# Two attentions of a fused two-block network: their loops over scores, weights and sums reordered

## The chip, the cores and the metric

The kernel runs on one core of a Trainium2 chip. The metric is the time of one execution on the device in microseconds (us), the median of several runs. TensorE (PE) multiplies matrices into eight PSUM banks, and its clock is granted at one of two levels, 1.2 or 2.4 GHz (0.50 and 1.00 in the rows). VectorE (DVE) and ScalarE (ACT) read and write PSUM and SBUF; GpSimd (POOL) works on SBUF here and issues some of the DMAs; SyncE (SP) streams the weights.

## The reference, cut to what matters

Everything is float32, for 512 tokens of width 1024. A first network of two layers (a recurrent mixer, then an attention with a window and sinks, each followed by a feed-forward and a gated input) feeds a second of two layers (the first of them with latent attention). Only these parts are touched:

```python
# attention with sinks: 16 query heads, 4 key heads, blocks of 128 queries, window of 128
logits = einsum('bnqhgd,bnkhd->bnhgqk', qb, kw) * (dh ** -0.5)     # own block and the one before
logits = where(valid, logits, -inf)
m = maximum(max(logits, axis=-1), sink)
probs = exp(logits - m[..., None])
denom = sum(probs, axis=-1) + exp(sink - m)
out = einsum('bnhgqk,bnkhd->bnhgqd', probs, vw) / denom[..., None]

# latent attention: 16 heads, q and k of width 96, v of width 64, blocks of 128 queries
s = einsum('bhqd,bkhd->bhqk', qi, k)                                # q scaled by 96 ** -0.5
s = where(kpos[None, :] <= qpos[:, None], s, -inf)
o = einsum('bhqk,bkhd->bqhd', softmax(s), v)
```

The sines and cosines of the first attention's rotation come from an input of positions, so they are computed in the kernel.

## The kernel before, in words

The order of the work is written out by hand, as one instruction stream for each engine, with semaphores between them. There is no scheduler: an engine does what stands next in its stream and waits there. TensorE's results take turns in two groups of four banks: `product` uses banks 0 to 3 (semaphores `product_full`, `product_done`), `small` banks 4 to 7 (`small_full`, `small_done`). Whoever empties a bank counts its `done` up, and the fifth use of a group waits for the first.

**Attention with sinks (stage `at`).** A unit is one block of queries for two of the 16 heads (`e` = 0, 1), so there are 32 units, n = u // 8 being the query block. Units 0 to 7 have only their own block of keys (128 columns a head), the others 256. In its turn u TensorE computes the scores of unit u, the transposes of unit u - LAG (LAG = 3) and the weighted sums of unit u - LAG - 1, each into the next small bank. DVE scales and masks the scores into SBUF (two instructions, L2102), takes the maximum (L2106), folds the sink in (L2109), and later (`at_scale`, L2083 to L2087) adds the exponential of the sink, inverts, and scales both heads' weights in place. ACT does the exponentials, copies the transposes out (two instructions) and then the sums. Four buffers of `temporary` hold the weights of four units.

**Before that stage (`ple2`, `norm3`, `at_in`).** `ple(2)` adds the gated input to the residual. Behind it on DVE stand nine instructions that reduce the rotation's angles (L2043 to L2053); they wait for the positions, whose DMA POOL issues (L673) only once `ple2` is done. Only then does DVE come to the reciprocal that the norm's spreading on TensorE waits for (L1831). `at_in` has 12 products of 512 columns (q and k), each followed by a sum of squares (`halves`) of the product before and a `turn` (the rotation's exchange) of the one before that. The last sum and the last two turns stand ahead of `token_major`, which computes the values (64 matmul rows of 256 columns in the trace). The stage `at` waits for the last rotation and for DVE's copies of the values (L2076).

**Latent attention (stage `mla`).** A unit is one block of queries of one head: 64 units, u = 4 hd + n, and n + 1 blocks of 128 keys. TensorE's turn u holds the scores of unit u and the transposes of unit u - 3; once the last block of a head is turned (n = 3), its four weighted sums follow at once (512, 384, 256 and 128 columns), behind a wait for ACT's four copies. All of it passes through the four small banks. DVE scales and masks the scores into `temporary` (L2283, over all keys), takes the maximum (L2286), negates it (L2287), and, one unit later, inverts the sum of the exponentials (L2293) and scales the weights (L2294). ACT does the exponentials, copies the transposes to `area_b`, and copies the head's sums to `normed`.

L741 is the helper that issues every matmul, L1065 and L1146 are the transposes of the two attentions, L1403 is the helper of all ACT instructions.

## Time and profile before

| | us |
|---|---|
| runs, median of 3 | 4471.97 (4466.77 to 4472.01) |
| profiled execution, whole | 4468.67 |
| its span, first to last instruction | 4466.8 |
| stage `at`, first scores to first product behind it | 97.2 |
| stage `mla`, the same | 166.2 |

TensorE is busy for 95% of the span, at a mean granted clock of 0.963. The two attentions are stretches in which it is less busy and its clock is lower; every other long stage is dense products. The stage times are differences of the starts at 1078.88 and 1176.06, and at 2406.08 and 2572.25.

### The profile page before, as it was taken

What the parts mean: (1) busy time and instruction counts of PE and PEld (TensorE: products, weight loads), DVE (VectorE), ACT (ScalarE), POOL (GpSimd) and SP (SyncE); (2) the same over time, 40 slices, a digit from 0 to 9 for tenths busy, and PEclk for the clock granted to TensorE, in tenths of its full rate; (3) what the DMA queues carried; (4) which work ended last, traced back from release to release, by engine and by line L of the source; (5) the groups of instructions that cost most, each with busy time, mean ns of one, the idle gap of its engine ahead of it and who ended that gap; (6) DMA issues with size and microseconds to landing.
All of it is one profiled execution on the core that took longest, in us unless ns stands there. A gap on an engine that the chain in (4) does not pass through costs nothing.

```text
span 4466.8 us, 40791 instructions
## 1 busy us (share of the span) xinstructions
PE 4263.6 (95%) x15992; PEld 2735.7 (61%) x15992; DVE 1573.6 (35%) x2918; ACT 693.5 (16%) x1468; POOL 1667.7 (37%) x1520
## 2 busy tenths in 40 slices
PE   7999999998999999999998799999999989989998
PEld 3444444445544444688843368888888346837887
DVE  4431110146511101344244534324432854454332
ACT  2321110023411100100023410001000231211000
POOL 0008888300088883244400024443443033003442
PEclk9999999998999999999999899999999889989999
DMA  3114334111053442222210022222222133112222
GB/s 115 47 64 181 146 147 154 72 64 38 34 183 146 150 152 70 71 85 83 87 61 29 1 76 85 85 85 81 89 83 88 38 101 85 33 38 76 88 87 71
DMA packets 125070, 387.45 MB, mean 87 GB/s; under 512 B 37648, under 2 KB 40720, under 8 KB 111440
## 3 DMA queue, kind: packets, MB, share of 16 engines
q1 hardware_dynamic: 109568, 302.56, 20.4%
q0 software_dynamic: 15312, 82.28, 4.8%
q8 instruction: 128, 2.10, 0.2%
q14 instruction: 62, 0.51, 0.0%
HBM read 376.40 MB, written 8.39 MB: 86 GB/s over the span
## 4 chain that ended last, share of the span: by engine, by line
PE 91%; DVE 5%; ACT 2%; issue 1%; DMA 0%; POOL 0%; DVEq 0%; POOLq 0%; ACTq 0%
PE bank L741 90%; DVE temporary L2498 1%; ACT temporary L1403 1%; DVE small_columns L2286 1%; DVE temporary L2283 1%; ACT normed L1403 0%; ACT area_b L1403 0%; DVE normed L1834 0%; DMA vector_columns<-in_vectors_dram 0%; DVE temporary L2102 0%; DVE small_columns L2106 0%; PE bank L1065 0%; PE bank L1285 0%; DVE area_a L2311 0%; DVE rstd L1849 0%
## 5 line engine op out<-in xcount | busy, mean ns | idle before, releaser
L741 PE MATMUL bank<-normed,weight_ring 128*128 128x512 f32 (+2 forms) x4080 | 1514.0, 528 | 17.4 <-DVE normed L1840 5.8
L741 PEld LDWEIGHTS bank<-normed,weight_ring 128*128 128x128 f32 (+1 forms) x4080 | 780.9, 193 | 699.3 <-issue 639.4
L741 PE MATMUL bank<-area_a,weight_ring 128*128 128x512 f32 (+1 forms) x1776 | 636.4, 515 | 8.2 <-issue 8.2
L741 PEld LDWEIGHTS bank<-area_a,weight_ring 128*128 128x128 f32 x1776 | 339.3, 192 | 282.0 <-issue 259.7
L691 POOL TENSOR_TENSOR area_b<-weight_ring 128x512 f32<-128x512 f32 (+1 forms) x68 | 84.2, 1238 | 1137.8 <-issue 567.3
L741 PE MATMUL bank<-area_b,weight_ring 128*128 128x256 f32 (+3 forms) x1616 | 500.0, 457 | 5.8 <-issue 2.8
L661 POOL TENSOR_SCALAR area_b<-area_b,small_columns 128x384 f32<-128x384 f32 x336 | 416.7, 1240 | 0.0
L741 PEld LDWEIGHTS bank<-area_b,weight_ring 128*128 128x128 f32 (+2 forms) x1616 | 302.9, 188 | 178.0 <-issue 147.0
L663 POOL TENSOR_TENSOR area_b<-area_b 128x384 f32<-128x384 f32 x336 | 333.9, 994 | 28.0
L741 PE MATMUL bank<-area_b 128*128 128x256 f32 (+2 forms) x1200 | 258.7, 378 | 16.3 <-ACT area_d L1403 16.3
L691 POOL TENSOR_TENSOR area_d<-weight_ring 128x512 f32<-128x512 f32 (+1 forms) x68 | 84.2, 1238 | 447.7 <-PE bank L741 422.8
L741 PEld LDWEIGHTS bank<-area_b 128*128 128x128 f32 (+1 forms) x1200 | 214.8, 196 | 51.4 <-ACT area_d L1403 16.9
L741 PE MATMUL bank<-area_b,area_d 128*128 128x256 f32 x1056 | 239.0, 379 | 0.0
L741 PEld LDWEIGHTS bank<-area_b,area_d 128*128 128x128 f32 x1056 | 200.6, 190 | 27.3
L1403 ACT ACTIVATE area_d<-area_d 128x512 f32<-128x512 f32 (+1 forms) x104 | 57.8, 563 | 918.4 <-DVE area_d L2184 918.4
L741 PE MATMUL bank<-normed,area_d 128*128 128x256 f32 (+2 forms) x1088 | 197.9, 339 | 0.2 <-issue 0.2
L741 PE MATMUL bank<-area_b,area_a 128*64 128x128 f32 (+11 forms) x640 | 161.6, 405 | 37.7 <-ACT area_b L1403 23.6
L638 POOL DMA_DIRECT2D area_b<-in_weights_dram x48 | 28.7, 597 | 411.1 <-PE bank L741 398.7
L2205 DVE SCALAR_TENSOR_TENSOR residual<-temporary,modulations,residual 128x256 f32<-128x256 f32 x64 | 45.3, 708 | 370.9 <-ACT temporary L1403 369.8
L741 PEld LDWEIGHTS bank<-normed,area_d 128*128 128x128 f32 (+2 forms) x1088 | 156.3, 171 | 24.4 <-issue 2.9
L1878 DVE TENSOR_TENSOR residual<-residual,bank 128x512 f32<-128x512 f32 x32 | 22.0, 688 | 418.9 <-PE bank L741 418.9
L1403 ACT ACTIVATE temporary<-bank 128x256 f32<-128x256 f32 (+1 forms) x136 | 59.0, 434 | 693.9 <-PE bank L741 693.9
(277 smaller groups left out, 4629.9 us busy)
## 6 DMA issues: line engine op xcount, KB each, us to landing
weight_ring<-in_weights_dram SPq DMA_DIRECT2D x387, 512.0 KB, 4.6
weight_ring<-in_weights_dram SPq DMA_DIRECT2D x56, 1024.0 KB, 4.8
area_b<-in_weights_dram POOLq DMA_DIRECT2D x48, 1024.0 KB, 5.3
area_b<-in_weights_dram POOLq DMA_DIRECT2D x48, 512.0 KB, 6.4
weight_ring<-in_weights_dram SPq DMA_DIRECT2D x40, 384.0 KB, 4.3
weight_ring<-in_weights_dram SPq DMA_DIRECT2D x24, 256.0 KB, 4.1
low_scratch<-area_d SPq DMA_DIRECT2D x16, 256.0 KB, 2.0
area_d<-low_scratch SPq DMA_DIRECT2D x16, 256.0 KB, 2.7
```

The lines of the kernel that those rows point to most:

```text
L638: po.dma_start(w[:, 0:k * P], io["weights"][b // TILE][:, b % TILE * P:]).then_inc(ada_landed[g % 3], 16)
L661: po.tensor_scalar(scaled, part, c, None, ALU.mult).then_inc(S("pool_step"), 1)
L663: i = po.tensor_tensor(total, total, scaled, ALU.add)
L691: po.tensor_tensor(s1, w21, w22, ALU.add).then_inc(S("pool_sum"), 1)
L741: i = pe.matmul(out, lhsT, rhs, start=start, stop=stop)
L1403: return act.activation(out, in_, func, **kw)
L1878: took(tt(X[:, k, :], X[:, k, :], pbank(m0 + k)[:, :], ALU.add), m0 + k)
L2205: return stt(x, part, g, x, ALU.mult, ALU.add)
L2283: stook(stt(w, sbank(s)[:, 0:(n + 1) * P], scale, C[:, CAT["causal"] + 512 - (n + 1) * P:CAT["causal"] + 512], ALU.mult, ALU.add), s)
L2286: own(dve.tensor_reduce(SM[:, o:o + 1], w, AX, ALU.max))
L2498: own(dve.reciprocal(r, r))
```

## The change

- **Latent attention.** It no longer uses the turns of the small banks. Scores have banks 4 to 7 (unit u in 4 + u % 4), transposes banks 0 and 1, the sums of a head bank 2 or 3, with semaphores of their own. The causal mask is added by DVE in the bank, on the 128 own keys only; the maximum is taken from the bank; ACT's exponential reads the bank and carries the factor 96 ** -0.5. The four weighted sums of a head are spread: one for each of the turns u = 4 hd + 8 to 4 hd + 11, between the scores and the transposes.
- **Attention with sinks.** LAG is 5 and there are eight buffers (four in `temporary`, four in `area_d`). Mask-adding, sink and the copy of the transposes are one instruction for both heads. DVE leaves at the reciprocal; the scaling by it is POOL's (two instructions a unit), between DVE and TensorE.
- **Before it.** The positions are loaded earlier on POOL's queue, the angles are computed by DVE inside `ple(2)` (ahead of its third block), the sines by ACT inside it (ahead of the fifth), the cosines by DVE ahead of the seventh. In `at_in` the last sum of squares and the last turns stand among the matmuls of the values.

```diff
-        LAG = 3
+        LAG = 5
...
+        def at_probs(v):
+            return (TM if v % 8 < 4 else D)[:, v % 4, :]
...
+        MLAG, MLA_OUT = 3, 8
+
+        def mla_scores(u):
+            return bank[4 + u % 4]
+
+        def mla_turned(u):
+            return bank[u % 2]
+
+        def mla_output(hd):
+            return bank[2 + hd % 2]
...
+            po.dma_start(B[:, 2, :].bitcast(I32), io["positions"]).then_inc(S("positions_landed"), 16)
...
-            po.dma_start(B[:, 2, :].bitcast(I32), io["positions"]).then_inc(S("positions_landed"), 16)
+
+            for v in range(32):
+                lo = 0 if v >= 8 else P
+                po.wait_ge(S("at_one_over"), v + 1)
+                for e in range(2):
+                    w = at_probs(v)[:, 256 * e + lo:256 * e + 256]
+                    i = po.tensor_scalar(w, w, at_column("one", v)[:, e:e + 1], None, ALU.mult)
+                i.then_inc(S("at_probs"), 1)
...
+            values = []
+            for k in range(DB):
...
+                if k == 0:
+                    square_sum(11)
+                    turn(10)
+                if k == DB - 2:
+                    turn(11)
...
-            for u in range(16 * NB + MLAG):
+            for u in range(16 * NB + MLA_OUT):
                 if u < 16 * NB:
                     hd, n = u // NB, u % NB
-                    s = small()
-                    mm(sbank(s)[:, 0:(n + 1) * P], A[0:96, hd, n * P:(n + 1) * P], B[0:96, hd, 0:(n + 1) * P], True, True,
-                       small_full)
-                if u >= MLAG:
+                    if u >= 4:
+                        pe.wait_ge(S("mla_exp"), u - 3)
+                    mm(mla_scores(u)[:, 0:(n + 1) * P], A[0:96, hd, n * P:(n + 1) * P], B[0:96, hd, 0:(n + 1) * P],
+                       True, True, S("mla_scored"))
+                if u >= MLA_OUT:
+                    hd, b = (u - MLA_OUT) // NB, (u - MLA_OUT) % NB
+                    if b == 0:
+                        pe.wait_ge(S("mla_copied"), NB * hd + NB)
+                        if hd >= 2:
+                            pe.wait_ge(S("mla_stored"), hd - 1)
+                    rows = slice(64 * (hd % 2), 64 * (hd % 2) + 64)
+                    mm(mla_output(hd)[rows, b * P:], A[:, 16 + 2 * b + hd // 8, hd % 8 * 64:hd % 8 * 64 + 64],
+                       B[:, 16 + 4 * (hd % 2) + b, b * P:], b == 0, b == NB - 1,
+                       S("mla_summed") if b == NB - 1 else None)
+                if 0 <= u - MLAG < 16 * NB:
                     v = u - MLAG
-                    hd, n = v // NB, v % NB
-                    s = small()
+                    n = v % NB
                     pe.wait_ge(S("mla_probs"), v + 1)
+                    if v >= 2:
+                        pe.wait_ge(S("mla_copied"), v - 1)
                     for b in range(n + 1):
-                        i = pe.transpose(sbank(s)[:, b * P:(b + 1) * P], TM[:, v % 4, b * P:(b + 1) * P], const("ident"))
-                    i.then_inc(small_full, 1)
-                    if n == NB - 1:
-                        o = small()
-                        for j in range(NB):
-                            sdone(pe, mla_small("turned", v - 3 + j))
-                        rows = slice(64 * (hd % 2), 64 * (hd % 2) + 64)
-                        for b in range(NB):
-                            mm(sbank(o)[rows, b * P:], A[:, 16 + 2 * b + hd // 8, hd % 8 * 64:hd % 8 * 64 + 64],
-                               B[:, 16 + 4 * (hd % 2) + b, b * P:], b == 0, b == NB - 1,
-                               small_full if b == NB - 1 else None)
+                        i = pe.transpose(mla_turned(v)[:, b * P:(b + 1) * P], TM[:, v % 4, b * P:(b + 1) * P], const("ident"))
+                    i.then_inc(S("mla_transposed"), 1)
...
+            def sines():
+                act.wait_ge(S("angles"), 1)
+                own(a(B[:, 0, :], B[:, 0, :], ACT.Sin))
+                own(a(B[:, 1, :], B[:, 1, :], ACT.Sin))
+                a(B[:, 1, :], B[:, 1, :], ACT.Square).then_inc(S("sines"), 1)
+
+            ple(2, sines)
...
-                        o = 2 * (u % 4) + e
-                        p = TM[:, u % 4, 256 * e + (0 if n else 128):256 * e + 256]
-                        a(p, p, ACT.Exp, bias=SM[:, o:o + 1], accum_out=SM[:, 8 + o:9 + o]).then_inc(S("at_exp"), 1)
-                        a(SM[:, 16 + o:17 + o], vec("at_sinks", 4 * g + 2 * e + half), ACT.Exp,
-                          bias=SM[:, o:o + 1]).then_inc(S("at_exp"), 1)
+                        p = at_probs(u)[:, 256 * e + (0 if n else 128):256 * e + 256]
+                        a(p, p, ACT.Exp, bias=at_column("max", u)[:, e:e + 1],
+                          accum_out=at_column("sum", u)[:, e:e + 1]).then_inc(S("at_exp"), 1)
+                    a(at_column("sink", u), at_column("sink", u), ACT.Exp).then_inc(S("at_exp"), 1)
-                    for e in range(2):
-                        cols = slice(256 * e + (0 if v >= 8 else 128), 256 * e + 256)
-                        i = a(B[:, 12 + v % 4, cols], sbank(s)[:, cols], ACT.Identity)
-                    stook(i, s)
+                    out, turned = (x.rearrange("p (e k) -> p e k", e=2)[:, :, 0 if v >= 8 else P:]
+                                   for x in (B[:, 12 + v % 4, :], sbank(s)[:, :]))
+                    stook(a(out, turned, ACT.Identity), s)
...
+            def stored(hd):
+                rows = slice(64 * (hd % 2), 64 * (hd % 2) + 64)
+                act.wait_ge(S("mla_summed"), hd + 1)
+                a(H[rows, hd // 2, :], mla_output(hd)[rows, :], ACT.Identity).then_inc(S("mla_stored"), 1)
+
+            for u in range(16 * NB + MLA_OUT):
+                    if u >= 4:
+                        act.wait_ge(S("mla_transposed"), u - 3)
+                    a(TM[:, o, 0:(n + 1) * P], mla_scores(u)[:, 0:(n + 1) * P], ACT.Exp, scale=scale, bias=SM[:, o:o + 1],
+                      accum_out=SM[:, 4 + o:5 + o]).then_inc(S("mla_exp"), 1)
+                if u >= MLA_OUT + NB and u % NB == 0:
+                    stored(u // NB - 3)
+                if 0 <= v < 16 * NB:
+                    hd, n = v // NB, v % NB
+                    act.wait_ge(S("mla_transposed"), v + 1)
+                    if v >= 8 and n == 0:
+                        act.wait_ge(S("mla_summed"), hd - 1)
+                    a(B[:, 16 + 4 * (hd % 2):17 + 4 * (hd % 2) + n, n * P:(n + 1) * P],
+                      mla_turned(v)[:, 0:(n + 1) * P].rearrange("p (b t) -> p b t", t=P), ACT.Identity)\
+                        .then_inc(S("mla_copied"), 1)
+            stored(15)
...
+            ple(2, {2: angles, 6: cosines})
...
+            def at_one_over(v):
+                dve.wait_ge(S("at_exp"), 3 * v + 3)
+                own(tt(at_column("sum", v), at_column("sum", v), at_column("sink", v), ALU.add))
+                dve.reciprocal(at_column("one", v), at_column("sum", v)).then_inc(S("at_one_over"), 1)
...
+                    band = C[:, CAT["band"] + lo:CAT["band"] + 256].unsqueeze(1).to_broadcast([P, 2, 256 - lo])
+                    stook(stt(w, scores, 0.125, band, ALU.mult, ALU.add), s)
+                    sinks = V[:, VAT["at_sinks"] + 4 * g + half:VAT["at_sinks"] + 4 * g + half + 3:2, 0]
+                    most = at_column("max", u)
+                    own(dve.tensor_reduce(most, w, AX, ALU.max))
+                    own(tt(most, most, sinks, ALU.max))
+                    own(tt(at_column("sink", u), sinks, most, ALU.subtract))
+                    ts(most, most, -1.0, None, ALU.mult).then_inc(S("at_minus_max"), 1)
...
-                    s, w = mla_small("scores", u), TM[:, o, 0:(n + 1) * P]
-                    sfull(dve, s)
-                    if u >= 4:
-                        sfull(dve, mla_small("turned", u - 4))
-                    stook(stt(w, sbank(s)[:, 0:(n + 1) * P], scale, C[:, CAT["causal"] + 512 - (n + 1) * P:CAT["causal"] + 512],
-                              ALU.mult, ALU.add), s)
-                    sdone(dve, s)
+                    w, own_keys = mla_scores(u)[:, 0:(n + 1) * P], mla_scores(u)[:, n * P:(n + 1) * P]
+                    dve.wait_ge(S("mla_scored"), u + 1)
+                    own(tt(own_keys, own_keys, C[:, CAT["causal"] + 384:CAT["causal"] + 512], ALU.add))
-                    ts(SM[:, o:o + 1], SM[:, o:o + 1], -1.0, None, ALU.mult).then_inc(S("mla_minus_max"), 1)
+                    ts(SM[:, o:o + 1], SM[:, o:o + 1], -scale, None, ALU.mult).then_inc(S("mla_minus_max"), 1)
```

TensorE's stream in the latent attention before, from the turn of the fourth scores to the end of the first head's sums (each matmul stands once here; in the trace a float32 one has two rows, a transpose one). `area_b,area_a 64x...` are the weighted sums, `constant_matrices,temporary` the transposes:

```order
L741 MATMUL bank7<-area_b,area_a 128x512 [waits small_done3]
L1146 MATMUL bank4<-constant_matrices,temporary 128x128 [waits mla_probs,small_done0]
...
L741 MATMUL bank5<-area_b,area_a 128x384 [waits small_done1]
L1146 MATMUL bank6<-constant_matrices,temporary 128x128 [waits mla_probs,small_done2]
L1146 MATMUL bank6<-constant_matrices,temporary 128x128 x3
L741 MATMUL bank7<-area_b,area_a 64x512 [waits small_done0,small_done2,small_done3]
L741 MATMUL bank7<-area_b,area_a 64x384
L741 MATMUL bank7<-area_b,area_a 64x256
L741 MATMUL bank7<-area_b,area_a 64x128
L741 MATMUL bank4<-area_b,area_a 128x512 [waits small_done0]
```

Now, the same place one head later, where the first head's sums stand:

```order
L755 MATMUL bank4<-area_b,area_a 128x128 [waits mla_exp]
L755 MATMUL bank2<-area_b,area_a 64x512 [waits mla_copied]
L1189 MATMUL bank1<-constant_matrices,temporary 128x128 [waits mla_copied,mla_probs]
L1189 MATMUL bank1<-constant_matrices,temporary 128x128
L755 MATMUL bank5<-area_b,area_a 128x256 [waits mla_exp]
L755 MATMUL bank2<-area_b,area_a 64x384
L1189 MATMUL bank0<-constant_matrices,temporary 128x128 [waits mla_copied,mla_probs]
L1189 MATMUL bank0<-constant_matrices,temporary 128x128 x2
L755 MATMUL bank6<-area_b,area_a 128x384 [waits mla_exp]
L755 MATMUL bank2<-area_b,area_a 64x256
```

The four sums in one piece, with the fourth next scores behind them, have become one sum behind each of four scores.

TensorE at the end of `at_in` before: `squares` is the last sum of squares, `area_a` the last turns, `weight_ring,normed` the first matmuls of the values.

```order
L741 MATMUL bank6<-squares,constant_matrices 128x512 [waits at_square,small_done2]
L741 MATMUL bank7<-area_a,constant_matrices 128x512 [waits at_scaled,small_done3]
L741 MATMUL bank4<-area_a,constant_matrices 128x512 [waits at_scaled,small_done0]
L741 MATMUL bank2<-weight_ring,normed 128x256 [waits product_done2]
L741 MATMUL bank3<-weight_ring,normed 128x256 [waits product_done3]
```

Now, from the fourth of the 32 value matmuls, and again from the 28th:

```order
L755 MATMUL bank1<-weight_ring,normed 128x256 [waits product_done1]
L755 MATMUL bank6<-squares,constant_matrices 128x512 [waits at_square,small_done2]
L755 MATMUL bank7<-area_a,constant_matrices 128x512 [waits at_scaled,small_done3]
L755 MATMUL bank2<-weight_ring,normed 128x256
...
L755 MATMUL bank4<-area_a,constant_matrices 128x512 [waits at_scaled,small_done0]
L755 MATMUL bank2<-weight_ring,normed 128x256
```

The last sum and the last-but-one turn moved behind an eighth of the values, the last turn behind seven eighths.

## Rows read from the trace of the kernel before

**Rows 1.** The page: shares of the chain that ended last.

```profile
PE 91%; DVE 5%; ACT 2%; issue 1%; DMA 0%; POOL 0%; DVEq 0%; POOLq 0%; ACTq 0%
```

**Rows 2.** Windows: length, then busy us of PE, PEld, DVE, ACT, POOL; clock, DMA.

```profile
1078.88:1176.06 97.18, 90.45 (x464) 63.39 (x465) 79.67 (x288) 73.39 (x288) 0.00 (x0) 0.82 0.00 1
2406.08:2572.25 166.17, 120.88 (x416) 56.94 (x417) 97.33 (x320) 72.89 (x208) 0.00 (x0) 0.88 0.00 1
2416.00:2425.10 9.10, 6.44 (x26) 3.23 (x27) 6.08 (x21) 4.48 (x13) 0.00 (x0) 1.00 0.01 2
2455.50:2467.50 12.00, 9.34 (x27) 4.16 (x27) 6.06 (x21) 4.50 (x13) 0.00 (x0) 0.75 0.01 1
1095.00:1110.00 15.00, 15.00 (x44) 9.02 (x43) 10.40 (x37) 8.62 (x36) 0.00 (x0) 0.50 0.00 0
```

**Rows 3.** Timeline, `ple2` and norm3: start, length, engine, line, [idle before].

```profile
881.92 0.69 DVE L1889 TENSOR_TENSOR temporary<-temporary,bank 128x512 f32<-128x512 f32 x1 [7.17 <-PE bank L741]
...
941.67 0.27 ACT L1403 ACTIVATE small_columns<-bank,vector_columns 128x4 f32<-128x4 f32 x1 [4.71 <-PE bank L741]
...
944.71 0.17 DVE L1831 RECIPROCAL small_columns<-small_columns 128x4 f32<-128x4 f32 x1
```

**Rows 4.** Timeline, the end of `at_in` and the first scores.

```profile
1042.25 7.03 PE L741 MATMUL bank<-normed,weight_ring 128*128 128x512 f32 x16
...
1055.18 2.04 PE L741 MATMUL bank<-area_a,constant_matrices 128*128 128x512 f32 x2 [1.93 <-DVE area_a L2063]
1061.15 2.05 PE L741 MATMUL bank<-area_a,constant_matrices 128*128 128x512 f32 x2 [3.93 <-DVE area_a L2063]
1062.99 15.17 PE L741 MATMUL bank<-weight_ring,normed 128*128 128x256 f32 x64
...
1076.90 1.72 DVE L2076 COPY area_a<-bank 128x256 f32<-128x256 f32 x4 [11.65 <-PE bank L741]
...
1078.88 1.24 PE L741 MATMUL bank<-area_a 64*128 64x128 f32 x16 [0.71 <-DVE area_a L2076]
```

**Rows 5.** Stage `at`: timeline, chain (start, length, what), and POOL's group.

```profile
1083.37 0.66 PE L1065 MATMUL bank<-constant_matrices,temporary 128*128 128x128 f32 x2 [3.26 <-DVE temporary L2087]
...
1105.67 3.05 PE bank L741 x8
1108.72 1.04 PE bank L1065 x4
...
1117.25 0.59 PE bank L1065 x4
1117.84 2.08 PE bank L741 x12
...
1164.82 0.81 PE L741 MATMUL bank<-area_a 64*128 64x256 f32 x3
...
1176.06 2.38 PE L741 MATMUL bank<-area_b,weight_ring 128*128 128x512 f32 x5 [0.67 <-ACT area_b L1403]
...
L661 POOL TENSOR_SCALAR area_b<-area_b,small_columns 128x384 f32<-128x384 f32 x336 | 416.7, 1240 | 0.0
```

**Rows 6.** Stage `mla`: timeline, then groups (count, busy us, mean ns, idle before).

```profile
2416.01 3.39 PE L741 MATMUL bank<-area_b,area_a 128*64 128x512 f32 x10 [1.46 <-ACT area_b L1403]
...
2419.45 0.69 DVE L2283 SCALAR_TENSOR_TENSOR temporary<-bank,constant_matrices 128x512 f32<-128x512 f32 x1 [2.60 <-PE bank L741]
...
2455.46 6.31 PE L741 MATMUL bank<-area_b,area_a 128*64 128x512 f32 x10 [1.46 <-ACT area_b L1403]
...
L2283 DVE SCALAR_TENSOR_TENSOR temporary<-bank,constant_matrices 128x512 f32<-128x512 f32 x16 | 11.1, 692 | 55.2 <-PE bank L741 55.2
...
L2286 DVE TENSOR_REDUCE small_columns<-temporary 128x1 f32<-128x512 f32 x16 | 11.0, 686 | 0.5
...
L2293 DVE RECIPROCAL small_columns<-small_columns 128x1 f32<-128x1 f32 x64 | 9.8, 153 | 0.4 <-ACT temporary L1403 0.4
...
L2283 DVE SCALAR_TENSOR_TENSOR temporary<-bank,constant_matrices 128x128 f32<-128x128 f32 x16 | 4.6, 286 | 0.8 <-PE bank L741 0.8
```

142 lines of the change are left out of this document (52 added, 90 removed).

## The prediction

> **What bounds the kernel now.** I read four views in this order. The chain of waits gives TensorE 91% of the span and DVE 5% [rows 1]: outside the attentions there is nothing for this change to shorten, and DVE's share is where to look. The windows by stage then price the two attentions: 97.2 us for the one with sinks, at a mean clock of 0.82, and 166.2 us for the latent one, at 0.88, with TensorE busy for 120.9 us of it, DVE 97.3 and ACT 72.9 [rows 2]. No engine fills the latent stage, so it is bound by waits. The timeline shows which: behind the fourth scores of a head TensorE runs ten rows in one piece for 3.39 us, eight of weighted sums and two of the next 512-wide scores [rows 6]. It was let in by ACT's copy after 1.46 us of idling, and DVE, whose next mask-add needs those scores, sat idle for 2.60 us in front of it. A head takes 9.10 us at the full clock and 12.00 where the same ten rows took 6.31 at a clock of 0.75 [rows 2, 6]. Last, the timeline of the two joints: DVE's reciprocal in norm3 comes 2.77 us after ACT's root [rows 3], and TensorE stops twice for a turn before it may begin the values [rows 4].
>
> **The change, part by part.**
>
> *The angles.* The root ends at 941.67 + 0.27 = 941.94; the reciprocal starts at 944.71, when DVE has done its nine instructions on angles [rows 3]. With these gone it starts at about 942.0: 2.7 us less. They now stand in `ple2`, where DVE idles for 7.17 us before each block [rows 3]; nine instructions at no more than the 0.69 of the mask-wide one there come to 6.2 [rows 3], so the idle time covers them. If it did not, the price would be their excess once. ACT gets sines and changes of table there; the covers of both are alike. POOL was free long before, so the earlier DMA of positions waits for nobody. I take 2.7, between 0 and 2.8.
>
> *The end of `at_in`.* Values take 15.17 us for eight steps of rows, 1.90 a step; a 512-wide product of two rows costs 0.86 to 0.88 (7.03 for 16, the first group ends with its drain) [rows 4]. The sixteen rows end at 1042.25 + 16 x 0.43 = 1049.1, a sum of squares and a turn behind them at 1050.8. From there: step one to 1052.7, the last sum of squares to 1053.6, then the turn waits for DVE as before and starts at 1055.18 [rows 4], ends at 1056.0; six steps to 1067.4, the last turn to 1068.3. DVE then needs 2.1 us for the last rotation and 1.72 for its four copies [rows 4], which end at 1072.2; they used to end at 1078.6. The scores of stage `at` start 6.4 us earlier. TensorE no longer waits for the second turn's 3.93 us, and the first one's 15 us of values cover the rest. What is late next is the rotation, now behind the last turn. Bounds: 4 (both waits gone and nothing else) to 7.2 (values at full clock throughout).
>
> *Attention with sinks.* TensorE is the bound through most of it: a unit with 256 keys costs 0.59 for transposes and 2.08 for sums and scores at the full clock, 1.04 and 3.05 at the lower one, where only half the sums stand [rows 5]. The change does not take a row from it. DVE loses two scalings and the doubled instructions, ACT one instruction in each of three places; neither was the bound until near the end. Fill: before, 4.5 us from the first scores to the first transposes, with 3.26 idle [rows 4, 5]. Now two more units of scores go in ahead, but the path has POOL's two scalings in it. Net 0.5 us less. Drain: from the last scores, 1164.82 + 0.81, to the product behind it at 1176.06 there are 10.4 us [rows 5]; work in them is four groups of transposes (2.4) and five of sums (5.1), and 0.7 for ACT's last copy. The longer queue lets it run through: 2.2 us less. Against that stands the clock. It was at its lower level from 1083 to 1117 though TensorE was never idle (15 us out of 15 busy at 0.50 in the middle of it), and was up in the first turn with eight rows of sums [rows 2, 5]. That turn now comes two units of scores later (LAG 5), each 1.0 us dearer at the lower clock: 2.0 us more. Sum 0.7 less.
>
> POOL's scaling of 128x256 has no row. A 128x384 one on POOL takes 1.24 us [rows 5], so two take under 2.48; against a unit of 2.67 it is hidden, with five units of lead. Below, in proportion, it is 0.83 each. I take 0.85.
>
> *Latent attention.* DVE works 9.10 - 2.60 = 6.50 us a head. Mask-adding shrinks from 692 to 286 ns in the widest unit, evenly less in the others (0.41 + 0.27 + 0.14): 0.81 less, so 5.70 [rows 6]. The maximum over the bank has no row; over SBUF it takes 686 ns, and a DVE instruction that reads the bank at the same width 692 [rows 6], so I price it alike; a tenth more would give 5.9. ACT has 4.5 to 4.6 a head [rows 2]. TensorE: above, the 6.44 busy us of a head at full clock [rows 2], drains included; below, 3.39 + 1.29 for the narrower scores (768 columns, by the 0.43 of a 512-column row) + ten transposes by 0.59 / 4 = 1.48 [rows 4, 5, 6], in all 6.16. I take 6.2, 1.55 a unit. TensorE becomes the bound, DVE close behind. Nothing waits for a whole head any more: the sums of a head start five turns after its last scores, and their copies come two turns earlier.
>
> Fill: until the turn of the first sum the loop goes by DVE, 0.5 + 7 x 5.70 / 4 = 10.5 us. Then 55 turns of 1.55: 85.3. Drain: behind the last turn come the last unit's maximum, exponential, scaling, four transposes, copy, the last head's sums (2.3) and their copy, in all 6.7. The fill leaves TensorE half idle, which is where its clock has fallen in this stage; I add 3 us for one such spell (the ten rows cost 2.9 more at the lower clock [rows 6]). Sum 105.5 instead of 166.2: 60.7 less.
>
> *Sum.* 2.7 + 6.4 + 0.7 + 60.7 = 70.5 us. The profiled execution took 4468.7, and the median of the runs is 3.3 above it. So 4398.2 for an execution like that one, 4401.5 for the median; I say 4401.
>
> **The rivals.**
>
> *The lower clock keeps coming back in the latent stage.* Seven of its sixteen heads now take 9.10 us or close to it, the others 10.4 to 12.1, and the slower ones have a clock of 0.75 to 0.83; one of each kind is in [rows 2]. If it did so in half the heads after the change, each would cost 6.2 + 2.9 + 1.29 = 10.4 instead of 6.2, and the time would be 4401 + 8 x 4.2 = 4435. For it: in stage `at` a TensorE that was never idle stayed at the lower level for over 30 us [rows 2, 5]. Against it: in the latent stage the clock fell where TensorE idled for waits, and these go; scores and sums now form an even stream of 640 columns a turn.
> The Trainium skill (TensorE: Matmul & The Clock Gate, section "A second HAM failure mode: psum-queue depth-cycling") says that a loop which goes through PSUM banks with short idle moments between its groups of matmuls has its clock swing between both levels; this loop does that, and by that rule this rival is the outcome. The stretch of stage `at` after 1117, also short groups over four banks, kept the full clock, which speaks against the rule here.
>
> *DVE and ACT in series.* DVE's reciprocal waits for the exponential of the unit before, and with it the next unit's mask-add is stuck. If each unit paid for it (mask 0.32, maximum 0.55, negation 0.2, exponential 0.65, inversion and scaling 0.5: 2.2 us), the 64 would take 141 and the whole 4401 + 40 = 4441. Against it: 64 such waits came to 0.4 us before [rows 6], and each unit still has the next one's mask and maximum between.
>
> *The clock rises early in stage `at`.* The rotation's idle is gone, and TensorE may start its units warm. Eight small units would gain 0.9 each and five large ones 1.3: 4387. Little speaks for it, since the first transposes still wait some 4 us.
>
> *Slower than before.* If the small matmuls of both attentions never let the clock rise, stage `at` pays from its thirteenth unit on 2 x 2.08 + 1.04 = 5.2 instead of 2.67, eighteen times: 46 us; the latent stage takes 16 x 10.4 + 12 = 178, 12 more than before; the joints give back 9. In all 4472 + 49 = 4521. It decides from the latent stage alone being at the lower level throughout (about equal to before); every unit of stage `at` beyond four makes it slower.
>
> **How the numbers follow.** The forecast has 0.75, the swinging clock 0.10, the series 0.06, the early clock 0.05, the slower case 0.03; 0.01 is left for a transfer or wait that I have not seen and that eats everything. The forecast's own range is 4388 to 4416: 5.70 a head as the pace and no spell would give 10 less, 6.44 four more, half the joints 5 more. To hold 8 in 10 with the two dearer cases near 4435, I say 4385 to 4434. A measurement of this kernel tells from no change about 0.2%, 9 us. Faster 0.96, same 0.01, slower 0.03.
>
> **What would show it.** Right: norm3's reciprocal within 0.2 us of the root; values starting before the last two turns, with one wait of 1.6 us; stage `at` 96 us long, with a low clock until its fifteenth turn; POOL's scalings under 1.0 us; a latent stage of 100 to 110 us at a clock above 0.95, TensorE idle under 5%, DVE at about 90%. Wrong: a clock near 0.75 in the latent stage, DVE idle before its reciprocals, or a maximum over the bank dearer than 0.75 us for 512 columns.

## The result and the profile after

The changed kernel takes 4398.37 us (median of 4 runs, 4395.47 to 4400.04) against 4470.55 us for the kernel before (4 runs): a ratio of 0.9841, 95% interval 0.9829 to 0.9854. I had said 4401. The profiled execution has a span of 4398.2 us, 68.6 less than before. Cut at five places that both programs pass, the difference is:

| stretch | before | after | forecast |
|---|---|---|---|
| start to norm3's root | 941.67 | 941.35 | 0 |
| root to first scores of `at` | 137.21 | 126.38 | -9.1 |
| `at` | 97.18 | 96.64 | -0.7 |
| `at_out` to `mla` | 1230.02 | 1230.99 | 0 |
| `mla` | 166.17 | 108.65 | -60.7 |
| `mla_out` to the end | 1894.55 | 1894.19 | 0 |

The sum is -0.32 - 10.83 - 0.54 + 0.97 - 57.52 - 0.36 = -68.60.

The page of the changed kernel gives the shares of the chain that ended last:

```profile
PE 94%; DVE 3%; ACT 2%; issue 0%; DMA 0%; POOL 0%; DVEq 0%; ACTq 0%; POOLq 0%
```

DVE went from 5% of the chain to 3 [rows 1]. The change is real: the whole interval of the ratio lies under 1. The windows of the two attentions, and behind them one head of the latent one (length, then busy us of PE, PEld, DVE, ACT, POOL, granted clock, DMA share, GB/s):

```profile
1067.73:1164.37 96.64, 91.79 (x465) 64.32 (x465) 62.80 (x224) 64.95 (x224) 53.29 (x64) 0.79 0.00 1
2395.36:2504.01 108.65, 105.50 (x416) 46.42 (x416) 86.31 (x320) 71.62 (x208) 0.00 (x0) 1.00 0.00 1
2410.64:2417.23 6.59, 6.59 (x27) 2.87 (x27) 5.65 (x23) 4.64 (x15) 0.00 (x0) 1.00 0.00 0
```

In `mla` TensorE is busy for 97% of the stage at the full clock; before it was 73% at 0.88 [rows 2]. Of the 57.5 us gained, 42.1 are idle time of TensorE (45.3 before, 3.2 now) and 15.4 are busy time, which shrank because no row runs at the lower clock any more. A head takes 6.59 us, and TensorE has no idle time in it. In `at` the mean clock has fallen from 0.82 to 0.79, and POOL has taken 53 us of work.

The joints, in the timeline of the changed kernel (start, length, engine, line, what, idle time before and its releaser):

```profile
941.35 0.26 ACT L1436 ACTIVATE small_columns<-bank,vector_columns 128x4 f32<-128x4 f32 x1 [4.71 <-PE bank L755]
941.65 0.18 DVE L1872 RECIPROCAL small_columns<-small_columns 128x4 f32<-128x4 f32 x1 [5.73 <-ACT small_columns L1436]
...
1038.85 7.03 PE L755 MATMUL bank<-normed,weight_ring 128*128 128x512 f32 x16
...
1051.78 1.10 PE L755 MATMUL bank<-area_a,constant_matrices 128*128 128x512 f32 x2 [1.60 <-DVE area_a L2108]
...
1052.72 10.52 PE L755 MATMUL bank<-weight_ring,normed 128*128 128x256 f32 x48
...
1063.08 1.02 PE L755 MATMUL bank<-area_a,constant_matrices 128*128 128x512 f32 x2
...
1066.07 1.41 DVE L2121 COPY area_a<-bank 128x256 f32<-128x256 f32 x4
...
1067.73 2.41 PE L755 MATMUL bank<-area_a 64*128 64x128 f32 x20 [1.91 <-DVE area_a L2121]
```

The reciprocal follows the root by 0.30 us instead of 3.04 [rows 3]. One turn is waited for, 1.60 us; the other, at 1063.08, has no wait. Of the two waits of 1.93 and 3.93 us [rows 4] the second is gone. A new one stands in front of the first scores, 1.91 us where it was 0.71 [rows 4], since the rotation and the copies come behind the last turn.

The first transposes of `at` on TensorE, the turn in which its clock rises, and POOL's scalings (in the view of one line: duration ns min/median/max):

```profile
1072.99 0.66 PE L1096 MATMUL bank<-constant_matrices,temporary 128*128 128x128 f32 x2 [1.47 <-POOL temporary L686]
...
1106.13 1.11 PE L1096 MATMUL bank<-constant_matrices,temporary 128*128 128x128 f32 x4
1107.18 1.97 PE L755 MATMUL bank<-area_b,area_a 128*64 128x128 f32 x8
1109.08 1.29 PE L755 MATMUL bank<-area_a 64*128 64x256 f32 x4
1110.29 0.66 PE L1096 MATMUL bank<-constant_matrices,temporary 128*128 128x128 f32 x4
```

```profile
L686 POOL TENSOR_SCALAR temporary<-temporary,small_columns x32: 597/924/927, 1071.7 to 1148.3; 128x256 f32<-128x256 f32 x24, 128x128 f32<-128x128 f32 x8
```

Four transposes take 1.11 us before that turn's sums and 0.66 behind it; in the kernel before, the chain has 1.04 and 0.59 for them [rows 5]. The low clock ends with the scores that start at 1109.08, 41.4 us into the stage. In the kernel before it ended with those at 1115.69, 36.8 us into it, also in the first turn with eight rows of sums:

```profile
1113.79 1.97 PE L741 MATMUL bank<-area_b,area_a 128*64 128x128 f32 x8
1115.69 1.56 PE L741 MATMUL bank<-area_a 64*128 64x256 f32 x4
```

POOL's scaling of 128x256 takes 924 ns.

In `mla`, first a stretch of TensorE's timeline, then DVE's groups over thirteen heads (count, busy us, mean ns, idle time before):

```profile
2443.43 0.33 PE L1189 MATMUL bank<-constant_matrices,temporary 128*128 128x128 f32 x1
2443.59 1.39 PE L755 MATMUL bank<-area_b,area_a 96*128 96x128 f32 x4
2444.91 0.44 PE L1189 MATMUL bank<-constant_matrices,temporary 128*128 128x128 f32 x2
2445.19 1.39 PE L755 MATMUL bank<-area_b,area_a 96*128 96x256 f32 x4
```

```profile
L2316 DVE TENSOR_TENSOR bank<-bank,constant_matrices 128x128 f32<-128x128 f32 x53 | 15.7, 296 | 9.5 <-PE bank L755 9.5
L2317 DVE TENSOR_REDUCE small_columns<-bank 128x1 f32<-128x512 f32 x13 | 9.0, 692 | 0.4
```

A turn is a group of transposes, then two rows of scores and two of one block's sums. The mask-add in the bank costs 296 ns, the maximum over the bank 692, and DVE waits 9.5 us in 85 for scores. Before, the waits in front of the widest unit's mask-add alone came to 55.2 us in the stage [rows 6].

### The profile page after: what moved, and what is told of

The parts are those of the page before. It is cut to its first block, busy times and chain, and to the rows that moved or that the text cites. A ratio compares the mean times of both kernels' runs of the same rounds, so it can differ in the third digit from the quotient of the medians.

```text
span 4398.2 us, 40701 instructions
## 1 busy us (share of the span) xinstructions
PE 4247.2 (97%) x15992; PEld 2725.3 (62%) x15992; DVE 1546.4 (35%) x2854; ACT 683.6 (16%) x1404; POOL 1722.9 (39%) x1584
## 4 chain that ended last, share of the span: by engine, by line
PE 94%; DVE 3%; ACT 2%; issue 0%; DMA 0%; POOL 0%; DVEq 0%; ACTq 0%; POOLq 0%
PE bank L755 92%; DVE temporary L2529 1%; PE bank L1189 1%; ACT normed L1436 0%; PE bank L1096 0%; DVE normed L1875 0%; DMA vector_columns<-in_vectors_dram 0%; ACT temporary L1436 0%; ACT area_b L1436 0%; DVE rstd L1890 0%; PE bank L1318 0%; DVE area_a L2342 0%; ACT squares L1436 0%; ACT L1436 0%; DVE temporary L2040 0%
## 5 line engine op out<-in xcount | busy, mean ns | idle before, releaser
L755 PE MATMUL bank<-area_b 128*128 128x256 f32 (+2 forms) x1200 | 258.6, 378 | 16.2 <-ACT area_d L1436 16.2
L755 PE MATMUL bank<-normed,area_b 128*128 128x256 f32 x704 | 166.3, 379 | 0.0
L755 PE MATMUL bank<-area_b,area_a 128*64 128x128 f32 (+11 forms) x640 | 148.8, 374 | 13.2 <-DVE area_b L2033 9.8
```

Of the source, the lines that this page charges most:

```text
L755: i = pe.matmul(out, lhsT, rhs, start=start, stop=stop)
```

## The experiments

Eleven of the twelve kernels below have the same instructions in front of norm3's root as the changed one (experiment 2 moves the angles), and yet this part took from 932.93 us in one of them to 941.35 in the changed kernel, each in its profiled execution, with the clock's low spells in other places. So a part worth a few us is read from the length of its stage, and the time of the whole kernel is the second witness.

**1. The latent part as before.**

```
-            for u in range(16 * NB + MLA_OUT):
+            for u in range(16 * NB + MLAG):
...
+                    if n == NB - 1:
+                        o = small()
+                        for j in range(NB):
+                            sdone(pe, mla_small("turned", v - 3 + j))
...
-                    own(tt(own_keys, own_keys, C[:, CAT["causal"] + 384:CAT["causal"] + 512], ALU.add))
+                    stook(stt(w, sbank(s)[:, 0:(n + 1) * P], scale, C[:, CAT["causal"] + 512 - (n + 1) * P:CAT["causal"] + 512],
+                              ALU.mult, ALU.add), s)
```

> The changed kernel with the latent attention alone put back: mask-add over the full width into SBUF, the four weighted sums of a head in one piece behind its last transposes, all in the four banks used in rotation. The joints and the attention with sinks stay changed. If the two attentions don't influence each other, the stage is 166 us long again instead of 108.6 and the time is 4398.4 + 57.5 = 4456, ratio to the kernel before 0.9967. Rival: part of the 57.5 us comes from TensorE entering the stage in a better state than before (it waits 0.88 us there); then the stage stays well under 166 (say 150) and the time under 4441.

Measured: 4457.48 us, ratio 0.9978 (0.9968 to 0.9987). Window of the stage:

```profile
2392.70:2561.24 168.54, 123.31 (x416) 57.98 (x417) 97.30 (x320) 72.88 (x208) 0.00 (x0) 0.86 0.00 1
```

The whole gain of the stage goes with its code; the rival is out. The low clock comes back too: the ten rows behind the fourth scores took 6.31 us in one head and 3.40 in the next.

**2. The joints as before.**

```
-            ple(2, {2: angles, 6: cosines})
+            ple(2)
...
-                if k == 0:
-                    square_sum(11)
-                    turn(10)
-                if k == DB - 2:
-                    turn(11)
```

> The changed kernel with the angles back in front of norm3's reciprocal, and the values of at_in back behind the last two turns. Both attentions stay changed. My steps say 2.7 us for the angles and 7.8 for the end of at_in, so that the first scores of the attention with sinks start 10.8 us later and the time is about 4409, ratio 0.9864. Rival: the joints' gain is given back at the start of the attention with sinks, because TensorE's clock falls there after the wait for the last rotation: with only 0.7 us of waiting there, as before, the clock would stay up for longer, the stage would be some us shorter than 96.6, and the time under 4404.

Measured: 4402.45 us, ratio 0.9855 (0.9838 to 0.9871). From the root to the first scores it is 138.25 us, 11.9 more than in the changed kernel, and the stage behind is 4.3 longer, not shorter:

```profile
1074.34:1175.30 100.96, 94.36 (x464) 65.72 (x465) 62.71 (x224) 64.83 (x224) 53.30 (x64) 0.78 0.00 1
```

The two add up to 16.2 us, of which the whole kernel shows 4.1: against them stand 5.3 us in front of the root (where DVE and ACT no longer have the angles) and 3.8 and 4.2 in the long stretches behind the two attentions, whose code is unchanged; `mla` took 1.1 more. The clock did fall later (7 us into the stage instead of in its first), but it also rose later, at 51 us instead of 41. The rival had the first half right and the second wrong. Its time, under 4404, did come true, but by the spells elsewhere and not by a shorter stage.

Against the kernel before, which differs from this one in the attention with sinks as well, the stage is 3.8 us longer (100.96 for 97.18). So behind the old joints the changed attention costs time.

**3. The attention with sinks as before.**

```
-        LAG = 5
+        LAG = 3
...
-                    at_one_over(u - 1)
+                    at_scale(u - 1)
```

> The changed kernel with the attention with sinks alone put back: transposes three turns behind the scores, the scaling on DVE, one instruction for each half in the mask-add and in ACT's copy. Theory: this part of the change is worth half a microsecond, since TensorE bounds the stage and its lower clock costs as much as the filled drain gives: stage 97 us against 96.6, low clock until the twelfth turn instead of the fourteenth, time 4399, ratio 0.984. Rival: the old form would pay for an earlier start of the scores with waits on DVE, and the stage is 100 us or more.

Measured: 4395.12 us, ratio 0.9836 (0.9821 to 0.9851).

```profile
1064.18:1163.23 99.05, 92.65 (x464) 64.77 (x465) 79.72 (x288) 73.36 (x288) 0.00 (x0) 0.79 0.00 1
```

In its stage the change is worth 2.4 us; the kernel's own time, 3 us lower than with the change, doesn't show it: 3.5 us less in front of the root and 4.2 less in the long stretch behind the stage outweigh it. The turns with the first eight sums, at a lag of three:

```profile
1099.09 1.97 PE L739 MATMUL bank<-area_b,area_a 128*64 128x128 f32 x8
...
1104.04 1.97 PE L739 MATMUL bank<-area_b,area_a 128*64 128x128 f32 x8
1105.94 1.13 PE L739 MATMUL bank<-area_a 64*128 64x256 f32 x4
```

The low clock ended 41.8 us into the stage, with a lag of five 41.4, which is not what I had expected: the first eight sums came two turns earlier, 34.9 us into the stage, but they and the next eight were still at the lower level.

**4. The mask-add in SBUF.** Only the mask, the scaling by 96 ** -0.5 and the exponential's source go back; TensorE's order stays.

```
-                    own(tt(own_keys, own_keys, C[:, CAT["causal"] + 384:CAT["causal"] + 512], ALU.add))
+                    own(stt(w, mla_scores(u)[:, 0:(n + 1) * P], scale,
+                            C[:, CAT["causal"] + 512 - (n + 1) * P:CAT["causal"] + 512], ALU.mult, ALU.add))
```

> The changed kernel, but in the latent attention the mask is added over the full width into SBUF and scaled there, and the exponential reads SBUF; the order on TensorE with sums by key block stays. Theory A (order gives the gain): DVE has 5.84 us a head now and gets 0.81 more, 6.65, against 6.59 of TensorE: 1 to 2 us longer for the stage, 110 us, time 4400. Theory B (the narrow mask-add in the bank gives a good part): DVE becomes the bound with its waits for the exponential showing, 7.2 us a head, stage 118 us, time 4408.

Measured: 4392.48 us, ratio 0.9832 (0.9817 to 0.9846).

```profile
2387.85:2497.71 109.86, 105.60 (x417) 46.34 (x417) 96.65 (x320) 73.60 (x208) 0.00 (x0) 1.00 0.00 1
```

Theory A: DVE gets 10.3 us more work and the stage 1.2. The narrow mask-add bought next to nothing in this kernel; the order on TensorE, with its separate banks, bought the other 56 us. No run tells the later sums from the separate banks.

**5. TensorE kept busy in the fill of the attention with sinks.** Seven products that nobody reads stand in front of four waits.

```
+            def busy(s, times):
+                for _ in range(times):
+                    mm(sbank(s)[:, :], const("turn"), A[:, 0, :], True, True, None)
+            busy(s0, 2)
             pe.wait_ge(S("at_rotated"), 12)
...
+                    if v < 2:
+                        busy(s, 2 - v)
                     pe.wait_ge(S("at_probs"), v + 1)
...
+                    if v == 0:
+                        busy(s, 2)
                     sdone(pe, at_small("turned", v))
```

> The changed kernel with seven products that nobody reads, each of two 512-wide rows, put on TensorE in front of its waits in the fill of the attention with sinks: two before the last rotation's, two and one before the first two groups of transposes, two before the first weighted sums. They add no more than 7 x 0.86 = 6 us, and most of it lies in waits of 1.9 + 1.5 + 0.5 + 1.8 us. Theory A (the clock falls for the idle of the fill): it stays at its upper level, or comes back with the first of them, and the stage is 15 us shorter, about 81 us, time 4383. Theory B (the small products themselves keep it low): the low clock covers the turns to about 41 us into the stage as before, and the stage is 97 to 99 us, time 4399.

Measured: 4383.53 us, ratio 0.9812 (0.9797 to 0.9826). The stage, and then TensorE's timeline in its fill:

```profile
1062.46:1146.33 83.87, 81.39 (x475) 56.72 (x475) 62.07 (x224) 64.26 (x224) 53.15 (x64) 0.98 0.00 1
```

```profile
1066.66 3.48 PE L755 MATMUL bank<-area_a,constant_matrices 128*128 128x512 f32 x4 [0.92 <-DVE temporary L2149]
...
1072.31 1.88 PE L755 MATMUL bank<-area_a,constant_matrices 128*128 128x512 f32 x4
1074.12 0.65 PE L755 MATMUL bank<-area_b,area_a 128*64 128x128 f32 x4
```

The clock fell for a moment (3.48 us for four rows that take 1.88 below) and was back before the first sums; it then kept the upper level through the very turns that had run at the lower one. 12.8 us for seven products: theory A, though the stage was forecast at 81 us. The low clock lasted some 4 us here and 40 in the changed kernel.

**6. Only the first two of them.**

```
+            pe.wait_ge(small_done[s0 % 4], s0 // 4)
+            busy(s0, 2)
             pe.wait_ge(S("at_rotated"), 12)
```

> The changed kernel with only the first two of the seven unread products: those in front of the last rotation's wait of 1.9 us, behind which the clock fell 0.6 us into the stage. Theory A (that wait alone makes it fall): the stage is as short as with all seven, about 83 us. Theory B (the waits of the fill behind it, 1.5 + 0.5 + 1.8 us, make it fall as well): the clock falls some us later, as where the values stood behind the turns and only 0.7 us were waited (it fell 6 to 8 us into the stage and stayed down until 51), and the stage is 96 to 101 us.

Measured: 4397.41 us, ratio 0.9847 (0.9833 to 0.986).

```profile
1065.01:1161.64 96.63, 90.78 (x464) 63.35 (x465) 62.77 (x224) 64.92 (x224) 53.14 (x64) 0.81 0.00 1
```

```profile
1070.27 0.66 PE L1103 MATMUL bank<-constant_matrices,temporary 128*128 128x128 f32 x2 [1.98 <-POOL temporary L686]
1070.93 1.22 PE L755 MATMUL bank<-area_a 64*128 64x128 f32 x4
...
1075.14 1.09 PE L755 MATMUL bank<-area_b,area_a 128*64 128x128 f32 x4 [1.81 <-ACT area_b L1443]
```

Theory B. The wait in front of the scores is filled, the granted clock is 1.00 until some 4.2 us into the stage, and it falls within the 1.98 us of idling in front of the first transposes. It rose again as in the changed kernel, 41 us into the stage. The fill's own waits suffice.

**7. The wide units first.**

```
+        def at_block(v):
+            return (v // 8 + 1) % NB
...
-                    n, g, half = u // 8, u // 2 % 4, u % 2
+                    n, g, half = at_block(u), u // 2 % 4, u % 2
```

> The changed kernel with the units of the attention with sinks in another order: the 24 units of 256 keys first, the 8 of 128 keys last. Theory A (the clock rises in the first turn with eight rows of sums, which now comes about 18 us earlier): low level to some 20 us into the stage; the turns that then run at the upper level save 10 us or more, and the last eight units stay up: stage 83 to 88 us, time about 4387. Theory B (the clock stays low for some 41 us whatever stands in the turns): the turns in that time are the dearer ones, at 5.2 us each, so that 8 of them are run in it instead of 11 or 12 and the rest stay to be done at the upper level: stage 97 to 101 us, time 4399 to 4403. Theory C: it falls again in the small units at the end, which take 3.67 instead of 1.9: 12 us more than A.

Measured: 4379.61 us, ratio 0.9806 (0.979 to 0.9822); stage 88.54 us, 8.1 shorter. The turns with eight sums:

```profile
1075.66 1.94 PE L759 MATMUL bank<-area_b,area_a 128*64 128x128 f32 x8 [2.03 <-ACT area_b L1440]
...
1080.58 1.97 PE L759 MATMUL bank<-area_b,area_a 128*64 128x128 f32 x8
...
1085.52 1.87 PE L759 MATMUL bank<-area_b,area_a 128*64 128x128 f32 x8
...
1088.97 1.09 PE L759 MATMUL bank<-area_b,area_a 128*64 128x128 f32 x8
```

The low level ends 25 us into the stage, in the third such turn. So it doesn't last a fixed time; B is out, and so is C, since the small units at the end kept the upper level. A had the direction, but said "the first turn" where it is the first to the third: the first in the kernel before, in the changed one and in experiment 6, the second in experiment 3, the third here and in experiment 2. Without unread products the clock never came back in this stage in a turn with four rows of sums. What decides between the first and the third turn stays open.

**8. The sums of a head in one piece**, in the turn of their first block.

```
-                    mm(mla_output(hd)[rows, b * P:], A[:, 16 + 2 * b + hd // 8, hd % 8 * 64:hd % 8 * 64 + 64],
+                    for b in range(turn_of, turn_of + 4 if turn_of % 4 == 0 else turn_of):
+                        mm(mla_output(hd)[rows, b * P:], A[:, 16 + 2 * b + hd // 8, hd % 8 * 64:hd % 8 * 64 + 64],
```

> The changed kernel with the four weighted sums of a head in one piece again, in the turn in which their first stands now; the narrow mask-add in the bank, the banks and the delay of eight turns stay. Theory A (each change between scores, sums and transposes costs TensorE some 0.1 us; the delay alone took the waits away): three changes a head fewer on each side of the sums, 6.2 to 6.3 us a head instead of 6.59, stage 103 to 105 us, time 4394. Theory B (spreading the sums feeds DVE evenly): DVE, with 5.84 us of work a head, waits behind the 2.1 us of sums, 7 us a head or more, stage 116 us, time 4406.

Measured: 4381.19 us, ratio 0.9808 (0.9793 to 0.9822).

```profile
2392.99:2489.65 96.66, 92.69 (x417) 53.47 (x417) 84.47 (x320) 68.77 (x208) 0.00 (x0) 1.00 0.00 1
```

5.71 us a head, better than theory A had it. DVE's mask-adds over 60 us of steady turns:

```profile
L2317 DVE TENSOR_TENSOR bank<-bank,constant_matrices 128x128 f32<-128x128 f32 x43 | 12.6, 293 | 0.0
```

No idle time stands in front of them, DVE was busy for 55.6 of the 60 us, and in these 60 us it waited for no other engine: it sets the pace now. So the delay of eight turns took the waits away, and spreading the sums cost 12 us.

**9. Values 128 columns wide.**

```
-                    mm(mla_output(hd)[rows, b * P:], A[:, 16 + 2 * b + hd // 8, hd % 8 * 64:hd % 8 * 64 + 64],
+                    mm(mla_output(hd)[:, b * P:], A[:, 16 + 2 * b + hd // 8, hd % 8 // 2 * P:hd % 8 // 2 * P + P],
```

> The changed kernel with the weighted sums over 128 columns of values (those of both heads of a pair) instead of 64; ACT reads the 64 rows of the bank that belong to the head, so that the output is the same, and the number of rows on TensorE too. Scores and sums then use the same columns of the array. Theory A (the 0.24 us a turn that the rows of TensorE don't explain is the change to a narrower part of the array): 0.1 to 0.2 us less a turn, stage 96 to 102 us, if DVE with 5.84 us a head allows it. Theory B (it is the change of operands, whatever their width): stage within 1 us of 108.6.

Measured: 4381.05 us, ratio 0.9807 (0.9792 to 0.9821). Stage, and two turns of TensorE:

```profile
2392.82:2488.78 95.96, 92.09 (x416) 58.41 (x416) 83.95 (x320) 69.17 (x208) 0.00 (x0) 1.00 0.00 1
```

```profile
2445.19 0.60 PE L1189 MATMUL bank<-constant_matrices,temporary 128*128 128x128 f32 x4
2445.62 1.25 PE L755 MATMUL bank<-area_b,area_a 96*128 96x512 f32 x4
2446.71 0.27 PE L1189 MATMUL bank<-constant_matrices,temporary 128*128 128x128 f32 x1
```

From the four rows' start to the next transposes' it is 1.09 us, where it was 1.32 with 64 columns (2443.59 to 2444.91 above), and twice the weights cost nothing. A head takes 5.65 us, with no wait in front of DVE's mask-adds here either. Theory A. Since DVE sets the pace here too, the 0.23 us a turn are the least that the passes cost.

**10. Scores over all 128 rows**, the values narrow again.

```
-                    mm(mla_scores(u)[:, 0:(n + 1) * P], A[0:96, hd, n * P:(n + 1) * P], B[0:96, hd, 0:(n + 1) * P],
+                    mm(mla_scores(u)[:, 0:(n + 1) * P], A[:, hd, n * P:(n + 1) * P], B[:, hd, 0:(n + 1) * P],
...
+                dve.memset(A[96:128, j, :], 0.0).then_inc(S("mla_q_ready"), 1)
```

> The changed kernel with the scores of the latent attention taken over 128 rows of the array instead of 96 (rows 96 to 127 of the queries are set to zero by DVE behind each rotation); the values stay 64 columns wide. Their number of rows is the same. With 128 columns of values the stage came down from 108.6 to 96.0. Theory A (any change of the part of the array that is used costs, rows as well as columns): some of it comes back here, stage 100 to 106 us. Theory B (it is the 64 columns alone): stage 108 to 109 us.

Measured: 4396.74 us, ratio 0.9845 (0.9832 to 0.9859).

```profile
2392.54:2501.15 108.61, 105.46 (x417) 46.38 (x417) 86.29 (x320) 71.55 (x208) 0.00 (x0) 1.00 0.00 1
```

108.61 as before: it is the 64 columns alone. By the Trainium skill (TensorEngine Tiling (Array Packing), section "Key Properties") a change of tiling mode drains TensorE; its section "Available Configurations" lists 128x64 as a mode apart from 128x128, and no mode of 96 rows. The times fit both, 0.23 us a turn for the columns and nothing for the rows; a drain as such can't be seen in these traces.

**11. Both gains together** (experiments 5 and 9, with the edits shown there).

> The changed kernel with all seven unread products in the fill of the attention with sinks, and with the values of both heads of a pair as 128 columns in the latent attention's sums. If the two gains (12.8 and 12.7 us in their stages) don't touch each other: stages of 84 and 96 us, time 4398.4 - 25.5 = 4373, ratio 0.979.

Measured: 4368.88 us (4 runs, 4367.19 to 4370.78), ratio 0.9783 (0.977 to 0.9796); stages of 83.87 and 96.02 us. They don't touch each other. It is the fastest of all kernels here, 29 us under the changed one.

**12. The scaling on POOL, and the sums in one piece, on top of it.**

```
-        MLAG, MLA_OUT = 3, 8
+        MLAG, MLA_OUT = 5, 10
...
+            for v in range(16 * NB):
+                po.wait_ge(S("mla_one_over"), v + 1)
+                po.tensor_scalar(mla_probs(v), mla_probs(v), mla_column("one", v), None, ALU.mult).then_inc(S("mla_probs"), 1)
```

> As the kernel with both gains, and in the latent attention also the sums of a head in one piece, and the scaling of the exponentials on POOL instead of DVE, with transposes five turns behind the scores and sums ten. DVE falls from 5.3 us of work a head to under 4, POOL takes some 4.5. Theory A (DVE bounds the latent stage at 5.65 us a head now): TensorE's rows, 2.15 for scores, 2.15 for sums and 1.16 for transposes, 5.46 in all, become the pace: 2 to 3 us less than 96 in steady turns, given back in part by the longer fill and drain, stage 93 to 97 us. Theory B (TensorE is already the bound at 5.65): nothing gained in steady turns, longer ends, stage 98 to 100 us. Theory C (DVE and POOL hinder each other): DVE's instructions get longer and the stage is over 100 us.

Measured: 4375.22 us, ratio 0.9802 (0.9789 to 0.9815); the latent stage takes 104.05 us. Its waits in 60 us of steady turns (who waited for whom, us, times, longest):

```profile
DVE bank L2338 <- PE bank L765: 16.3, 9, 1.9
...
PE bank L765 <- ACT area_b L1458: 6.2, 10, 1.4
```

None of the three: no instruction of DVE got longer (its mask-add 285 ns, its maximum 692), but a new wait stands in TensorE's turn, for ACT's copy in front of the four sums, though these stand two turns behind the head's last transposes as in experiment 8. A head takes 6.17 us, 0.48 of them idle on TensorE in front of these sums. In ACT's stream the copy now stands right behind the exponential of a widest unit, which had itself waited 0.49 us for DVE. Several things were changed at once, so which of them makes that copy late stays open. And with DVE at 32.5 us in 60 the pace was not better: whether TensorE alone could go under 5.65 us a head wasn't settled.

## Why the prediction was right

In the whole 70.5 us were forecast and 68.6 measured. The two joints and the latent attention were understood, with errors of 1.7 us and 3.2 us that point in opposite directions; the attention with sinks was not.

**The angles**: 2.7 forecast, 2.74 measured. The nine instructions fitted into an idle stretch of `ple2`, as said.

**The end of `at_in`**: 6.4 forecast, 7.75 measured, from 1042.25 to 1078.88 before and from 1038.85 to 1067.73 after. These two make 10.5 of the 10.8 us up to the first scores; the other 0.3 lie between them. The chain ran as worked out up to the wait for the first turn (to 0.0 us). The values were mis-sized: I read 1.90 us a step from a row whose first 7 us ran at a clock of 0.83, behind the wait of 3.93 that the change removes; six steps took 10.36 us, 1.73 each. That is 1.0 us; the rest is DVE's copies, 1.41 for 1.72.

**Attention with sinks**: 0.7 forecast, 0.54 measured, and that is luck: the sum came out, its terms didn't. TensorE idled 1.9 us less (4.85 for 6.73), and its rows took 1.3 us more. The fill did not get shorter: the first transposes come 5.26 us into the stage, 4.49 before, since POOL's two scalings (0.6 us each) lie in the path. The low clock did end later than before, as I had said, but the reason that I gave, "That turn now comes two units of scores later (LAG 5)", is the step that failed: with the lag back at three (experiment 3) that turn is early again and the clock still rises after 41.8 us. What the part is worth depends on what stands in front of it, which I had not thought of: 2.4 us gained behind the new joints (experiment 3), 3.8 lost behind the old ones (experiment 2). And I left the thing that mattered out of the sum: a clock which falls in the fill's waits and which, without unread products, rose in none of the small turns. It costs 12.8 us, and seven unread products buy it back (experiments 5 to 7).

**Latent attention**: 60.7 forecast, 57.5 measured. That the stage was bound by waits, and that TensorE would become the bound, held: 97% busy. Four terms were off, and they cancelled in part. "I take 6.2, 1.55 a unit" is the one that failed: it is 6.59 and 1.65. The bounds that I had, 6.16 and 6.44, were both made of rows from the old order, in which a head passes to 64 columns and back once; in the new one each turn does, for 0.23 us (experiments 8 to 10). Where it doesn't, a head needs no more than 5.65, so my number was too high for the rows and too low for the order. Over 56 turns (I had counted 55) it makes 7.0 us too little. Against it the fill took 8.5 instead of 10.5, and the spell of low clock, 3 us, never came. The drain was 7.9 for 6.7. So 7.0 - 2.0 - 3.0 + 1.2 = 3.2. The maximum over the bank was priced right, 692 ns, and DVE's work in a head too, 5.65 us busy for 5.70; since the head is longer, DVE was busy for 79% of the stage and not the 90% that I had given as a sign.

**The rivals.** The swinging clock: 1.00 throughout the stage, in the changed kernel and in every variant that kept the delayed sums but for a spell near its start in some (0.98). I had named it as the outcome by the rule of the Trainium skill's page TensorE: Matmul & The Clock Gate (section "A second HAM failure mode: psum-queue depth-cycling"), and that was misread for the new order: the rule is about short idle moments between groups of matmuls, and this loop has none in a head (6.59 us busy of 6.59), so no run here speaks against it. The loop before, which idled for 2.7 of 9.1 us in a head, did swing between 0.75 and 1.00 [rows 2]. DVE and ACT in series: such a wait came once, with 0.4 us. Low clock in both attentions, and the rise at the start of `at`: neither came by itself, though experiment 5 shows that the second was to be had.

## What to carry to other kernels

Where a stage is bound by waits, put the work that depends on a whole group several turns behind it; that, with banks of its own for each kind of product, was worth 56 of 57.5 us here, and the narrower mask-add 1.2, on an engine that was not the bound. In the order of experiments 8 and 9, where DVE sets the pace, it should be worth more; no run shows it. Then look at what the new order made the matmul engine change between, and at its clock from the first wait of the stage on: an unread product in a wait is cheap (an estimated 6 us of rows, 7 x 0.86, for 12.8 gained), and so are 64 columns of values that nobody reads (12.7 us gained).

## What the hardware showed that I had not expected

- TensorE stayed at the lower clock for 31 us of turns in which it had no idle time (1077.9 to 1109), with four rows of sums a turn, and in every kernel without unread products it rose only in turns with eight. The same turns with four kept the upper clock where it was up when they began (experiment 5).
- Passing between products that fill 128 columns of the array and products that fill 64 costs TensorE at least 0.23 us a turn, without any idle time in the records: the 1.39 us of such a group hide it. Taking all 128 columns costs no more than taking 64. Going from 96 to 128 rows changes nothing.
- DVE's maximum over 128x512 takes 692 ns from a bank and took 686 from SBUF [rows 6]; POOL's scaling of 128x256 takes 924 ns.
- Code that was the same took 932.9 to 941.4 us in different programs up to the same point. The low spells of the clock fall in other places: the windows from 100 to 200 us have 0.93 in the changed kernel and 0.98 in that of experiment 4. There is one profiled execution of each, so how much of it would differ between two executions of one program isn't known.
